# Splitting the output weights during the q/k/v projections instead of during the gate projections

## The reference

```python
shift, scale, gate = adaln_params(c, ada_w[i], ada_b[i])          # silu(c) @ w + b
h = rms_norm(x, norm_g[i]) * (1.0 + scale) + shift
branch = attention_branch(h, ...) or pool_branch(h, ...)
x = x + gate * branch
...
def attention_branch(...):
    q, k, v, g = jnp.split(h @ w_in, ...)
    q = partial_rope(rms_norm(q, q_norm_g), positions)
    k = partial_rope(rms_norm(k, k_norm_g), positions)
    o = banded_sink_attention(q, k, v, sinks)
    return (o * jax.nn.silu(g)) @ w_out
```

## Time and profile before

| | |
|---|---|
| time, median of 3 runs | 1537.94 us (1537.39 to 1540.11) |
| the profiled execution | 1540.15 us, of which the span of the profile is 1538.4 us |
| PE busy with matmuls | 93% of the span |
| DVE, ACT, POOL busy | 58%, 35%, 25% |
| q/k/v tiles | first projection at 43.2 us, last from 370.17 us |
| gate chunks | 376.08 us to 581.14 us |

### The profile page before, as it was taken

How to read it: one execution, slowest core, us unless ns; L and a number is a source line. 1 busy time by engine, 2 the same in 40 slices (tenths; PEclk the granted TensorE clock), 3 DMA queues, 4 the chain that set the end, 5 groups by cost and what they waited for, 6 DMA issues and landing times.

```text
span 1538.4 us, 20207 instructions
## 1 busy us (share of the span) xinstructions
PE 1435.4 (93%) x7240; PEld 1210.9 (79%) x7240; DVE 890.7 (58%) x1524; ACT 538.0 (35%) x1270; POOL 386.1 (25%) x551
## 2 busy tenths in 40 slices
PE   1789999999899997789999999899999999999999
PEld 1577777788678786778888888688888888888887
DVE  7766677665434446787777775535456452645522
ACT  2433344333301115775556564322222222222200
POOL 2333333312222222454555555320000000000000
PEclk9999999999989998999999999999999999999999
DMA  8644555534987686766767765941111552112142
GB/s 309 212 165 160 197 191 191 193 121 160 345 309 275 261 321 220 268 245 232 263 251 277 274 240 194 334 126 41 55 42 62 171 193 74 42 55 75 49 150 82
DMA packets 96787, 285.62 MB, mean 186 GB/s; under 512 B 10768, under 2 KB 40496, under 8 KB 87088
## 3 DMA queue, kind: packets, MB, share of 16 engines
q1 hardware_dynamic: 87760, 250.74, 45.3%
q0 software_dynamic: 8928, 33.59, 6.2%
HBM read 196.22 MB, written 88.08 MB: 185 GB/s over the span
## 4 chain that ended last, share of the span: by engine, by line
PE 68%; DMA 9%; DVE 9%; issue 5%; ACT 4%; POOL 3%; SPq 1%; ACTq 0%; DVEq 0%; POOLq 0%
PE po_f_ps L1843 23%; PE po_y_ps L1859 11%; PE at_y_ps L1415 9%; PE qk_proj L667 7%; PE ga_g_ps L933 6%; PE at_o_ps L1399 5%; PE at_s_ps L1371 3%; DMA ga_ada<-in_ada_w 3%; DMA values_split<-qk_late 2%; PE at_tr L1381 2%; DMA po_xn<-x_mid_t 1%; POOL qk_rq L306 1%; ACT at_pr L1191 1%; POOL qk_acc L297 1%; DMA ga_raw<-in_attn_w_gate 1%
## 5 line engine op out<-in xcount | busy, mean ns | idle before, releaser
L1843 PE MATMUL po_f_ps<-po_ht,po_w 128*128 128x512 f32 x1536 | 348.9, 389 | 0.0
L1843 PEld LDWEIGHTS po_f_ps<-po_ht,po_w 128*128 128x128 f32 x1536 | 288.1, 188 | 60.1 <-DVE po_ht L1705 0.3
L667 PE MATMUL qk_proj<-qk_w_qkv,qk_ht 128*128 128x512 f32 x1152 | 281.9, 401 | 14.2 <-DVE qk_ht L460 8.2
L667 PEld LDWEIGHTS qk_proj<-qk_w_qkv,qk_ht 128*128 128x128 f32 x1152 | 216.9, 192 | 60.9 <-DVE qk_ht L460 9.3
L1415 PE MATMUL at_y_ps<-at_zt,at_w 128*128 128x512 f32 x768 | 197.0, 398 | 6.2 <-DVE at_x L1304 6.2
L1859 PE MATMUL po_y_ps<-po_zt,po_w 128*128 128x512 f32 x768 | 174.7, 389 | 0.0
L1859 PEld LDWEIGHTS po_y_ps<-po_zt,po_w 128*128 128x128 f32 x768 | 144.1, 188 | 29.9
L1415 PEld LDWEIGHTS at_y_ps<-at_zt,at_w 128*128 128x128 f32 x768 | 137.3, 189 | 31.4 <-issue 7.4
L1692 DVE TENSOR_TENSOR po_w<-po_raw,po_w 128x1024 fp32r<-128x1024 f32 x48 | 58.8, 1225 | 129.2 <-ACT po_w L1626 129.2
L1147 POOL TENSOR_SCALAR_AFFINE_SELECT at_pt<-at_ph 128x512 fp32r<-128x512 f32 x128 | 83.6, 676 | 187.6 <-ACT at_ph L1198 187.6
L306 POOL TENSOR_TENSOR qk_rq<-qk_mq,qk_half 128x8 f32<-128x8 f32 (+1 forms) x48 | 71.2, 1484 | 189.1 <-DVE qk_mq L487 189.1
(11 more groups left out here) (168 smaller groups left out, 2013.0 us busy)
## 6 DMA issues: line engine op xcount, KB each, us to landing
at_w<-out_weight_split SPq DMA_DIRECT2D x32, 1024.0 KB, 6.3
queries_t<-qk_late SPq DMA_DIRECT2D x16, 1024.0 KB, 4.2
ga_ada<-in_ada_w POOLq DMA_DIRECT2D x64, 256.0 KB, 4.5
at_qt<-queries_t SPq DMA_DIRECT2D x16, 1024.0 KB, 8.1
ht_split<-qk_ht SPq DMA_DIRECT2D x6, 2048.0 KB, 9.6
values_split<-qk_late SPq DMA_DIRECT2D x16, 768.0 KB, 4.9
at_vs<-values_split SPq DMA_DIRECT2D x16, 768.0 KB, 4.9
qk_late<-in_ada_w SPq DMA_DIRECT2D x16, 512.0 KB, 6.1
```

Source lines behind the costliest of these rows:

```text
L667: last = nc.tensor.matmul(proj[:, b * BANK:(b + 1) * BANK], ht[:, s % 2, m, k, t * P:(t + 1) * P], w_qkv[:, w, k, b * BANK:(b + 1) * BANK] ...
L1843: last = nc.tensor.matmul(f_ps[:, bank(j, h), :], w[:, i % 2, a, k, :], ht[:, h, m, k, :], start=(n == 0), stop=(n == 3 * KC - 1))
```

## The change

The eight pieces of `w_out` are split in tiles 4 to 11 of the q/k/v stage, one in each tile. The three raw buffers serve as source, high half and low half. SP has at the top of tile `n` the store of piece `n` - 5 (`store_out`) and the load of piece `n` - 4 (`load_out`), ahead of all that it issues in the tile; ACT has the high half behind `evict_k`, DVE the low half behind `normalise(n, 2)`, each as the last work of the tile. The gate stage loses loads, halves and stores of these pieces; POOL issues no store any more. The first load of a gate weight waits for the last of the stores. The numbering of the ring behind it shifts, and the two semaphores of the folded weights of the attention stage are merged with two others, which counts the same events under other names.

```diff
@@ qkv_stage, SP
+        def load_out(d):
+            sp.wait_ge(w_lo, ITEMS + d)
+            sp.dma_start(raw[:, OUT_RAW, :], w_out[d].rearrange("p k c -> p (k c)")).then_inc(wo_loaded, 16)
+
+        def store_out(d):
+            sp.wait_ge(w_lo, ITEMS + d + 1)
+            sp.dma_start(wo_d[d], raw[:, OUT_HI:OUT_LO + 1, :]).then_inc(wo_stored, 16)
...
         for n in range(NB + 1):
+            if 0 <= n - FIRST_OUT - 1 < KC:
+                store_out(n - FIRST_OUT - 1)
+            if 0 <= n - FIRST_OUT < KC:
+                load_out(n - FIRST_OUT)
             if n < NB and n % 2 == 0:
                 store_ht(n // 2)
@@ qkv_stage, ACT
+        def out_high(d):
+            act.wait_ge(wo_loaded, 16 * (d + 1))
+            wait(act, wo_stored, 16 * d)
+            nc.scalar.activation(raw[:, OUT_HI, :].bitcast(F32R), raw[:, OUT_RAW, :], ACT.Copy).then_inc(w_hi, 1)
...
             if n > 0:
                 evict_k(n - 1)
+            if 0 <= n - FIRST_OUT < KC:
+                out_high(n - FIRST_OUT)
@@ qkv_stage, DVE
+        def out_low(d):
+            dve.wait_ge(w_hi, ITEMS + d + 1)
+            nc.vector.tensor_tensor(raw[:, OUT_LO, :].bitcast(F32R), raw[:, OUT_RAW, :], raw[:, OUT_HI, :], ALU.subtract).then_inc(w_lo, 1)
...
                 normalise(n, 2)
+            if 0 <= n - FIRST_OUT < KC:
+                out_low(n - FIRST_OUT)
@@ gate_stage
-    ITEMS = 2 * KC
+    ITEMS = KC
...
     def load(sp, i):
-        wait(sp, w_lo, ITEM0 + i - RAW + 1)
-        src = w_gate[i] if i < KC else w_out[i - KC]
-        sp.dma_start(raw[:, (RING0 + i) % RAW], src.rearrange("p k c -> p (k c)")).then_inc(raw_loaded[(RING0 + i) % RAW], 16)
+        if i == 0:
+            sp.wait_ge(qk["wo_stored"], 16 * KC)
+        sp.wait_ge(w_lo, ITEM0 + max(i - RAW + 1, 0))
+        sp.dma_start(raw[:, (RING0 + i) % RAW], w_gate[i].rearrange("p k c -> p (k c)")).then_inc(raw_loaded[(RING0 + i) % RAW], 16)
...
-        def store_out(d):
-            pool.wait_ge(w_lo, ITEM0 + KC + d + 1)
-            pool.dma_start(wo_d[d], wo[:, :, :].bitcast(F32)).then_inc(wo_stored, 16)
...
-            if out_piece(q) is not None:
-                hi(act, KC + out_piece(q))
...
-            if out_piece(q) is not None:
-                lo(dve, KC + out_piece(q))
```

More of the change, by code:

```diff
@@ L77, in build @@
         qk = qkv_stage(nc, sem, dims, weights, xt, c_col, positions, ada_w, ada_b, norm_g, attn_w_qkv, attn_q_norm, attn_k_norm,
-                       ht_d, qt_d, kt_d, vs_d, ident, c_silu)
-        ga = gate_stage(nc, sem, dims, weights, qk, attn_w_gate, attn_w_out, ada_w, ada_b, norm_g, ht_d, sg_d, wo_d, c_silu,
+                       attn_w_out, ht_d, qt_d, kt_d, vs_d, wo_d, ident, c_silu)
+        ga = gate_stage(nc, sem, dims, weights, qk, attn_w_gate, ada_w, ada_b, norm_g, ht_d, sg_d, c_silu,
                         gate0, mod1)
@@ L730, in qkv_stage, with gate_stage @@
     return {"sync": sync, "gpsimd": gpsimd, "scalar": scalar, "vector": vector, "tensor": tensor, "last_round": last_round, "ht": ht,
-            "items": ITEMS, "ring": ring_at(ITEMS), "hx_done": hx_done, "proj_done": proj_done, "qtr_done": qtr_done, "mx_done": mx_done, "act_ev": act_ev,
+            "items": ITEMS + KC, "wo_stored": wo_stored, "ring": ring_at(ITEMS), "hx_done": hx_done, "proj_done": proj_done, "qtr_done": qtr_done, "mx_done": mx_done, "act_ev": act_ev,
             "dve_ev": dve_ev, "k_lo": k_lo, "ht_stored": ht_stored, "stored": (q_stored, k_stored, v_stored)}
-def gate_stage(nc, sem_of, dims, weights, qk, w_gate, w_out, ada_w, ada_b, norm_g, ht_d, sg_d, wo_d, c_silu, gate0, mod1):
+def gate_stage(nc, sem_of, dims, weights, qk, w_gate, ada_w, ada_b, norm_g, ht_d, sg_d, c_silu, gate0, mod1):
     KC, NB, D = (dims[n] for n in ("KC", "NB", "D"))
@@ L772, in g_bank @@
         return g_ps[:, (q + 2) % 4, :]
-    def out_piece(q):
-        return (q - KC) // 3 if q >= KC and (q - KC) % 3 == 0 and (q - KC) // 3 < KC else None
     def ada_by(q):
@@ L812, in store @@
                          sg[:, :, :, :].rearrange("p n k t -> p n (k t)")).then_inc(sg_stored, 16)
-        for i in range(RAW + 2, KC + RAW):
+        for i in range(RAW + 2, ITEMS):
             load(sp, i)
@@ L820, in sync @@
                     load_h(sp, q // KC + 1)
-            if out_piece(q) is not None and KC + out_piece(q) + RAW < ITEMS:
-                load(sp, KC + out_piece(q) + RAW)
             if q == SLOTS - KC:
@@ L847, in gpsimd @@
                 load_ada(n)
-            if out_piece(q - 1) is not None:
-                store_out(out_piece(q - 1))
     def hi(act, i):
@@ L1017, in attend_stage, with wg_split, wv_split @@
     fold_loaded, wg_loaded, fold_stored = ring("fold_loaded", 3), ring("wg_loaded", 2), ring("fold_stored", 2)
-    fold_hi, fold_lo, wg_hi, wg_lo, fold_done, fold_out = (sem(n) for n in (
-        "fold_hi", "fold_lo", "wg_hi", "wg_lo", "fold_done", "fold_out"))
+    fold_hi, fold_lo, fold_done, fold_out = (sem(n) for n in ("fold_hi", "fold_lo", "fold_done", "fold_out"))
+    def wg_split(f):
+        return f * (PAIRS + 1) + 1
+    def wv_split(u):
+        return wg_split(u // PAIRS) + u % PAIRS + 1
     LAST = UNITS + BEHIND
@@ L1064, in load_fold @@
         if pair == 0:
-            wait(sp, wg_lo, f - 1)
+            if f >= 2:
+                sp.wait_ge(fold_lo, wg_split(f - 2))
             sp.dma_start(wg_raw[:, f % 2], w_group[GC * f:GC * (f + 1)].rearrange("c p n -> p c n")).then_inc(wg_loaded[f % 2], 16)
-        wait(sp, fold_lo, u - 2)
+        if u >= 3:
+            sp.wait_ge(fold_lo, wv_split(u - 3))
         sp.dma_start(wv_raw[:, u % 3], wvt[GC * f:GC * (f + 1)][:, :, pair * ROWS:(pair + 1) * ROWS].rearrange("c p n -> p c n")).then_inc(fold_loaded[u % 3], 16)
```

33 lines of the change are left out of this document (14 added, 19 removed).

## The result

The changed kernel took 1556.84 us (median of four runs, 1554.41 to 1558.46), the kernel before 1538.16 on the same chip: a ratio of 1.0119, 95% interval 1.0104 to 1.0134, or 18.7 us slower. 1554.4 was forecast, with a range of 1538 to 1563. The profiled execution of after is its fastest (1554.41, span 1552.7); that of before was above its median (span 1538.4), so the spans lie only 14.3 apart. A second profile of the changed kernel has a span of 1554.7.

What follows compares the result with a forecast made beforehand. Pairs of q/k/v tiles were taken as bound almost evenly by PE and a loop through the values' store and DVE's program; 26.3 lost less 9.9 regained added 16.4 to 1540.15, 1556.6, less 2.2 for the median: 1554.4 us, range 1538 to 1563.

Steps and rivals of the forecast that it cites:

- DVE's low half costs its full price in each tile: q/k/v stage: DVE's low half, 1.2 us, eight times directly ahead of `low_k`, with no gap to take it up.
- faster, 1529: Rival 3: DVE's low half falls into waiting time, q/k/v pays next to nothing, gate stage's 9.9 us stay; chance 0.13.
- The transfers ahead of the values cost 4.1 us in tiles 6, 8 and 10: q/k/v stage: 1.5 MiB more ahead of the values' store in SP's queue is added time, 4.1 us per tile.
- the transfers don't delay the values: Rival 2: what stands ahead in SP's queue need not land first, the 4.1 is gone; 1538 us, chance 0.14.
- The clock adds 0.8 in a pair: q/k/v pairs: slow clock behind PE's odd-tile wait makes PE lose 2.0 us at the next `spread` instead of 1.2.
- Tiles 5 and 6 lose 4.4: q/k/v stage, tiles 5 and 6: 1.2 + 1.2 + 2.0 = 4.4 us, with 1.2 for tile 4's load alone.
- PE waits 6 us for the eviction at an odd tile: q/k/v stage: PE's odd-tile wait for DVE's eviction of round 1 becomes 0.7 + 4.1 + 1.2 = 6.0 us.
- The gate stage gives 9.9 back: Gate stage: shorter waits for sums and less slow clock, 5.3, 1.2, 2.6 and 0.8, together 9.9 us.
- the first wait: Gate stage, at 423.05: a shorter queue for `ada_w` removes PE's 2.46 us wait and 2.8 of slow clock, 5.3 us.
- the second: Gate stage's longest wait, 3.3 us: piece 0's low half ahead of the sixteenth addition goes, 1.2 us.
- The wait at 504.57: Gate stage: a low half, 1.2 of the wait's 1.35 us, and 1.4 of slow clock behind it go, 2.6 us.
- the gate stage gives nothing back: Rival 4: `ada_w` rows are late for their own four buffers and the clock falls again; 1564 us, chance 0.07.

Runs made afterwards that it cites:

- the gate part alone: Changed kernel's gate stage, but in q/k/v only one piece loaded, split in mid tile 4 and stored eight times in odd tiles: 1538.33 us, 0.9998 of the kernel before.
- the kernels before with halves: Kernel before, each gate-stage hidden-state block loaded in two halves: 1537.77 us; the same with pieces two to eight split over 8 columns only: 1534.49 us.
- With halves: Changed kernel, each 4 MiB hidden-state block of the gate stage loaded in two halves, after a round's second and fourth chunk: 1544.50 us, 1.0060 of the kernel before.
- the spare store under way: Changed kernel with six splits in mid even tiles, plus a spare 1 MiB load and a POOL store held until chunk 15's matmuls are done: 1535.10 us.
- the kernel with splits in the middle and halves: Changed kernel with six splits in mid even tiles and gate-stage hidden-state blocks loaded in two halves: 1528.81 us, 0.9944 of the kernel before.

## Why the prediction was right, and where it was not

The total was right, slower by 1.2% for the cause named: both costs in the q/k/v stage are real, and taking either out gives time back. That it was right to 2.4 us is luck, since an error of 7.4 us on one side met one of 6.8 on the other. Point by point:

- *The high half costs nothing.* Right, shown by leaving it out.
- *DVE's low half costs its full price in each tile.* Right in the changed kernel: 1.13 us on the chain, twice in a pair. By itself, in the kernel without transfers in even tiles, it cost 9.5 us, but as 1.6 in a pair and as much again where the clock fell. The rival in which it falls into idle time ("faster, 1529") fell. That time exists, but in the middle of even tiles; the kernel with six splits there showed it.
- *The transfers ahead of the values cost 4.1 us in tiles 6, 8 and 10.* Right in kind, too large in size. The copy of v came 20.8 us after the keys' issue in tile 6 (184.94 to 205.72), before 17.5 (184.32 to 201.78): 3.3. The whole of the cost without low halves was 3.6 a pair (4.8, 2.2 and 3.7; 3.3 to 3.5 by POOL's reciprocals). It came as a later issue of the values and not as a later landing behind their issue. The figure by the ceiling in the Trainium skill (DMA: Bandwidth & Descriptors, Bandwidth), 3.6, was nearer than mine. The rival "the transfers don't delay the values" fell.
- *The clock adds 0.8 in a pair.* Here the step failed. The slow clock is there (7.95 us instead of 5.72), but the loop over ACT, DVE and POOL is as late as PE, so it adds nothing: 3.3 + 2 x 1.13 = 5.6 is what that loop got longer (5.5, 5.3 and 5.7 by POOL's reciprocals), and what the pairs lost on average (5.95, 4.9, 5.5). Forecast were 7.3. It is not free everywhere: without a wait for the values it made two pairs 1.6 us longer.
- *Tiles 5 and 6 lose 4.4.* They lost 2.5. The load alone cost nothing measurable: 0.1 us in the kernel without low halves.
- *PE waits 6 us for the eviction at an odd tile.* Missed in form: 2.94 there, and some 2 for ACT's eviction in front of it, 4.9 together in tile 7. I had followed only one of the two evictions.
- *The gate stage gives 9.9 back.* Wrong: 3.1 and 2.3 us in the two profiles, 1.9 with the gate part alone, and nothing measurable in the time. Of its terms the first wait vanished, but a wait of 2.54 us for a gate weight at 427.62 took over part of it in this profile (in others with the same gate stage it is 1.0 to 2.2, so partly chance, and where it is short the first wait is still 0.2 to 1.2); the second is right (3.3 to 2.05, 1.2 forecast); the third, *"The wait at 504.57"*, failed. I had put its 1.35 us down to a low half, and VectorE's additions did stand behind it with their data there. (Part of the wait is the store of the gates: in the kernels before with halves, leaving the low half out took it from 1.69 to 0.92 us only.) What I took for free was that the data would still be there. The removed store had been under way in POOL's queue when these loads were issued and had held back SP's store of the gates; without it two loads land 5.5 and 6.4 us later. I had written of the stores that they "lay beside PE's work".
- *The rival "the gate stage gives nothing back"* was right on the gate stage, for another reason than it gave, and had too high a total, since the q/k/v stage cost 18.9 and not 26.3.

With halves, so that the loads no longer meet 6 MiB, the removal does give 10.2 us: 3.2 for seven splits and 7.1 for the first split and the transfers. The forecast's 9.9 had 3.8 for low halves (1.2 + 2.6) and 5.3 for the shorter queue at the first wait. As a price for what the pieces cost the stage it was good; as a forecast of what their removal gives back it lacked what the removal sets free to be late next.

What stays open: why POOL's loads moved nothing in their first 4 us behind SP's transfers. How the 7.1 us fall on the first split and on the pieces' loads and stores wasn't tried either. And the reading by packets rests on the traces; no run changed the size of the hidden state's packets alone.

## What to carry to other kernels

Idle buffers are not idle time: eight splits with their transfers cost 18.9 us at the ends and starts of eight tiles, and 1.8 with six of the splits in the middle of tiles, where their engines wait, and most of the transfers in odd tiles. When you take transfers away, list what they held back; a store that nobody waits for can decide beside which other transfer a load has to share. And two causes in one place hide each other: removing the pieces alone gave nothing in time, the halves alone nothing, both together 9 us.

## What the runs showed of the hardware

- Two loads of 256 KB from POOL's queue, issued 0.5 and 1.4 us behind 6 MiB in SP's, landed in 13.3 to 13.4 and 16.9 to 17.0 us in the seven kernels where POOL's queue was empty at that moment, and in 7.9 and 10.6 or 8.1 and 9.2 in two where a 1 MiB store was under way in it. The Trainium skill (DMA: Bandwidth & Descriptors, Queues, rings and completion order) says that each engine goes round robin, packet by packet, between the queues that have work. Once the loads moved, the traces agree: 107 packets of SP's to 97 of POOL's in 2 us beside the store of the gates, 28 to 32 beside the hidden state. But with packets of 4 and 33 KB in SP's queue that left POOL 0.33 MB in the one case and 0.08 in the other. In the first 4 us behind their issue the loads moved nothing, which this rule does not tell.
- A backlog can show in the issuing engine. With 1.5 MiB more ahead of it, SP's issue of the load of x took 5.27 to 6.21 us instead of 2.92 to 3.04, and the issue of the hidden state in the gate stage took 0.91 and 1.28 us beside the 1 MiB store and 0.50 without.
- 2 MiB at a time leave room: the loads of the same place landed in 7.5 and 7.3 us in the kernel with splits in the middle and halves, where only the store of the gates was ahead.
- The length of a wait did not tell what the clock costs behind it. From the fifth sum to the sixth, with four chunks between them, it is 22.7 us where no wait stands ahead. Behind waits of 4.63 to 4.68 us it is 24.4 in the changed kernel and 25.0 to 26.0 in the seven other profiles that have this wait. Behind 1.35 us in the kernel before it is 24.4 too, behind 1.69 in the kernel before with halves 26.0, and behind 1.34 with the spare store under way 22.8, at full clock. The windows of the changed kernel, columns as above:

```profile
520.00:524.00 4.00, 4.00 (x13) 3.22 (x13) 1.11 (x2) 0.00 (x0) 1.10 (x2) 0.63 0.66 196
524.00:528.00 4.00, 4.00 (x19) 3.31 (x18) 0.30 (x1) 0.60 (x1) 0.00 (x0) 1.00 0.02 7
```
